# MLP products of a three-layer fp32 kernel by quarters: seven block products instead of eight

## The reference

```python
def squared_relu_mlp(h, w1, w2):
    return jnp.square(jax.nn.relu(h @ w1)) @ w2

mod = (c_act @ ada_w[layer] + ada_b[layer])[:, None, :]
sh_a, sc_a, gt_a, sh_m, sc_m, gt_m = jnp.split(mod, 6, axis=-1)
...
h = modulate(rms_norm(x, mlp_norm[layer]), sh_m, sc_m)
x = x + gt_m * squared_relu_mlp(h, mlp_w1[layer], mlp_w2[layer])
```

## Time and profile before

| what | value |
|---|---|
| three runs | 2585.17, 2585.69, 2588.85 us; median 2585.69 |
| the profiled execution | 2587.35 us, span 2585.6 us |
| mean granted TensorE clock over the span | 0.969 of full |
| TensorE busy | 2444.9 us (95%) |
| VectorE busy | 823.2 us (32%) |
| ScalarE busy | 465.4 us (18%) |
| mlp1 of layer a | first L901 at 381.32, first L959 at 615.50 |
| mlp2 of layer a | first L959 at 615.50, last sum of a chunk followed by the first L393 at 847.34 |

### The profile page before, as it was taken

One profiled execution on the slowest core, in us unless ns is written; L12 is line 12 of the kernel. 1 busy time (PEld: TensorE's weight loads), 2 busy tenths in 40 slices (PEclk: granted clock), 3 DMA queues, 4 the chain that ended last, 5 costly groups with the idle time before them and its releaser, 6 DMA issues. The chain is left out here.

```text
span 2585.6 us, 22377 instructions
## 1 busy us (share of the span) xinstructions
PE 2444.9 (95%) x8264; PEld 1216.3 (47%) x8264; DVE 823.2 (32%) x1835; ACT 465.4 (18%) x995; POOL 42.9 (2%) x50
## 2 busy tenths in 40 slices
PE   6999899999999999989999999999999899998886
PEld 4444544444444645554444444464554643343332
DVE  4444432112122436653211213138642411110104
ACT  2232211110000324441211100021231200000001
POOL 0000000000000000000000000000000000000000
PEclk9999799999999999989999999999999899999998
DMA  8443213333433111112433433341003569999995
GB/s 341 158 168 147 98 65 130 130 130 130 169 157 130 57 65 50 49 74 98 163 130 132 172 151 130 130 163 65 33 1 130 230 266 427 426 426 425 424 422 205
DMA packets 45426, 452.29 MB, mean 175 GB/s; under 512 B 7784, under 2 KB 7784, under 8 KB 20240
## 3 DMA queue, kind: packets, MB, share of 16 engines
q1 hardware_dynamic: 37616, 435.64, 42.0%
q0 software_dynamic: 6528, 12.17, 1.3%
q10 hardware_dynamic: 1184, 3.19, 0.3%
HBM read 444.54 MB, written 18.39 MB: 179 GB/s over the span
## 5 line engine op out<-in xcount | busy, mean ns | idle before, releaser
L959 PE MATMUL ps<-big,ring 128*128 128x512 f32 x1024 | 448.9, 596 | 3.9 <-PEq L871 1.8
L901 PE MATMUL ps<-hT,ring 128*128 128x512 f32 x1024 | 444.3, 594 | 0.0
L959 PEld LDWEIGHTS ps<-big,ring 128*128 128x128 f32 x1024 | 192.6, 191 | 245.9 <-issue 245.9
L901 PEld LDWEIGHTS ps<-hT,ring 128*128 128x128 f32 x1024 | 193.9, 191 | 237.9 <-issue 236.6
L2572 PE MATMUL ps<-ring,big 128*64 128x512 f32 (+1 forms) x768 | 233.3, 614 | 25.2 <-issue 15.3
L512 PE MATMUL ps<-hT,ring 128*128 128x512 f32 x384 | 175.0, 607 | 2.1 <-ACT hT L429 2.1
L2572 PEld LDWEIGHTS ps<-ring,big 128*64 128x64 f32 (+1 forms) x768 | 85.2, 151 | 144.3 <-issue 131.0
L1653 PE MATMUL ps<-hT,ring 128*128 128x512 f32 x320 | 142.4, 600 | 2.7 <-DVE big L2035 1.7
L2572 PE MATMUL ps<-big 128*64 128x512 f32 (+1 forms) x352 | 130.0, 604 | 6.6 <-ACT big L2633 3.3
L207 DVE SCALAR_TENSOR_TENSOR tmp<-ring,cact,tmp 128x512 f32<-128x512 f32 (+1 forms) x192 | 131.6, 685 | 6.8
L856 DVE TENSOR_TENSOR mod<-ps,vec 128x4 f32 (+1 forms) x16 | 2.6, 162 | 367.4 <-PE ps L214 367.4
(11 more groups left out here) (433 smaller groups left out, 2506.6 us busy)
## 6 DMA issues: line engine op xcount, KB each, us to landing
ring<-in_stream SPq DMA_DIRECT2D x99, 2048.0 KB, 8.4
ring<-in_gate SPq DMA_DIRECT2D x17, 2048.0 KB, 29.2
ring<-in_up SPq DMA_DIRECT2D x16, 2048.0 KB, 25.2
ring<-in_down SPq DMA_DIRECT2D x15, 2048.0 KB, 27.4
big<-in_up SPq DMA_DIRECT2D x9, 2048.0 KB, 25.2
big<-in_down SPq DMA_DIRECT2D x8, 2048.0 KB, 27.1
big<-in_gate SPq DMA_DIRECT2D x7, 2048.0 KB, 24.8
hT<-in_down SPq DMA_DIRECT2D x5, 2048.0 KB, 26.5
```

The lines of the kernel that those rows point to most:

```text
L901: last = pe.matmul(m.ps[:, j, :], w[:, k, j * P:(j + 1) * P], m.hT[:, k, :], start=(k == 0), stop=(k == KT - 1))
L959: last = pe.matmul(m.ps[:, bank(half, j), :], w[:, k, j * P:(j + 1) * P], hid[:, 8 * c + k, :], start=(c == 0 and k == 0), stop=(c == 3 an ...
```

## The change

Both products are computed by the Strassen-Winograd scheme on quarters. The two operands are cut in four quarters each; eight products of quarters become seven, and sums of quarters are formed before and after. In the names of the code the quarters of the weights are a11, a12, a21, a22, those of the rows b11, b12, b21, b22; S1, S2, S4 and a changed a21 are sums of weight quarters, T1, T2, T4 and a changed b12 are sums of row quarters; P1 to P7 are the seven products.

In mlp1 the first chunk of w1 is computed as before. Each of the other seven chunks is two pairs; a pair makes two hidden tiles f and g. Each of its seven products is four products of the code with a moving operand of 256 columns (`product`, L937). The sums of rows are formed once, those of weights (S1, S2, a21, S4, 512 elements per partition each) on VectorE for each pair, in place for a21 in the ring. VectorE joins the seven results from PSUM in seven additions of 256 elements. ScalarE copies P1 out of PSUM and does Relu and Square in place on quarters. The eight instructions of a modulation chunk are spread over the two pairs. The loop over four rounds is written out.

In mlp2 a step is one k of a chunk: seven products of two products of the code each, 256 columns, summed in seven banks over the 16 steps of a half. VectorE forms the sums of step s+1 during step s (256 elements each; eight instructions per step in the first half, seven in the second), with two sets of buffers. At the end of a half `outputs` joins the banks in seven additions of 512 elements and applies gate and residual in eight instructions of 256 elements (`joined`). The tiles are then squared in the order 2, 3, 0, 1. Buffers for all this are `oT`, `rs`, and parts of `tmp` and `hT`.

The diff, cut to its core:

```diff
-def square_rows(m, act, sq, scale, j, freed, sqd):
+def square_rows(m, act, sq, scale, j, freed, sqd, tile=None):
+    f = j if tile is None else tile
...
+                def product(name, a, b):
+                    out = m.ps[:, bank[name], 0:H]
+                    for k in range(4):
+                        ins = pe.matmul(out, a[:, k, :], b[:, k, :], start=(k == 0), stop=(k == 3))
+                    ins.then_inc(prod, 1)
...
+                for i, (c, q) in enumerate(pairs):
+                    if i:
+                        pe.wait_ge(p1_ok, i)
+                    product("P1", a11, b11)
+                    pe.wait_ge(s12_ok, i + 1)
+                    if i:
+                        pe.wait_ge(u2_ok, i)
+                    product("P6", s2, t2)
...
+                    product("P5", s1, t1)
+                    if q == 0:
+                        modulation_rows(c - 1)
...
+                    product("P7", a21, b12)
...
+                    product("P2", a12, b21)
...
+                    product("P4", a22, t4)
...
+                    product("P3", s4, b22)
+                    if q == 1:
+                        pe.wait_ge(prod, PRODUCTS * (i + 1))
+                        pe.sem_inc(m.free[chunk1(c)[0]], 1)
+                modulation_rows(7)
...
+                for i, (c, q) in enumerate(pairs):
+                    dve.wait_ge(p1_ok, i + 1)
+                    dve.wait_ge(prod, done + 2)
+                    dve.tensor_tensor(u2, p1, ps("P6"), ALU.add).then_inc(u2_ok, 1)
+                    ada(c, 4 * q, 4 * q + 1)
...
+                    if i + 1 < len(pairs):
+                        sums_a(*pairs[i + 1])
...
+                    dve.tensor_tensor(hid[:, f, H:T], u4, ps("P3"), ALU.add).then_inc(c12, 1)
+                    if i + 1 < len(pairs):
+                        sums_b(*pairs[i + 1], i + 1)
+                    ada(c, 4 * q + 3, 4 * q + 4)
...
+    steps = [(half, c, k) for half in range(2) for c in range(4) for k in range(4)]
+                    def product(name, a, b):
+                        for q in range(2):
+                            ins = pe.matmul(m.ps[:, bank[name], q * H:(q + 1) * H], a[:, q * P:(q + 1) * P], b,
+                                            start=(first and q == 0), stop=(final and q == 1))
+                        ins.then_inc(prod, 1)
...
+                def sums(s):
+                    if s >= 2:
+                        dve.wait_ge(prod, PRODUCTS * (s - 1))
...
+                    if c == 3 and k == 3:
+                        outputs(half)
+                for j in range(4, 7):
+                    squares(j)
```

More of the change, by code:

```diff
@@ L887, in _ @@
             def _(pe):
-                pe.sem_inc(relu, 4)
-                pe.sem_inc(mod_done, 1)
-                keep_busy(m, pe, 5, 7)
[L891 to L908, removed]
@@ new lines, in _ @@
+                keep_busy(m, pe, 5, 7)
+                chunk, full, v = ring_chunk(m, at)
+                pe.wait_ge(full, v)
+                w = chunk.rearrange("p (k n) -> p k n", k=8)
+                for j in range(4):
+                    for k in range(KT):
+                        if j == 0:
+                            pe.wait_ge(h_ok, k + 1)
+                        last = pe.matmul(m.ps[:, j, :], w[:, k, j * P:(j + 1) * P], m.hT[:, k, :],
+                                         start=(k == 0), stop=(k == KT - 1))
+                    last.then_inc(mm, 1)
@@ L910, in _, with squared @@
+                modulation_rows(7)
             @block.scalar
             def _(act):
-                act.sem_inc(sq, 2)
-                shift_rows(act, outs, hs, h_ok)
[L914 to L921, removed]
+                def squared(f, h, n):
+                    part = hid[:, f, h * H:(h + 1) * H]
+                    act.activation(part, part, ACT.Relu).then_inc(flat, 1)
+                    act.wait_ge(flat, n)
+                    act.activation(part, part, ACT.Square)
@@ new lines, in joined @@
+                def joined(f, h):
+                    for q in range(2):
+                        x = m.xT[:, f + q, h * H:(h + 1) * H]
+                        ins = dve.scalar_tensor_tensor(x, cres[:, q * H:(q + 1) * H], gate[:, f + q:f + q + 1], x, ALU.mult, ALU.add)
+                        c1.n += 1
+                        ins.then_inc(chn, 1)
+                        if f % 4 == 2 and h == 0 or f % 4 == 0 and h == 1:
+                            dve.wait_ge(chn, c1.n)
+                            dve.sem_inc(added, 1)
+                    dve.wait_ge(chn, c1.n)
@@ new lines, in squares @@
+                def squares(j):
+                    if 1 <= j <= 6:
+                        add_squares(dve, sq1, j, sqd, freed)
+                        if inner is not None:
+                            add_squares(dve, sq2, j, sqd2, freed2)
+                sums(0)
+                for s, (half, c, k) in enumerate(steps):
+                    if s + 1 < len(steps):
+                        sums(s + 1)
+                    i = 4 * half + c
+                    n2 = at2 + 2 * i + 1
+                    if k == 0:
+                        dve.wait_ge(m.full[n2 % RING], 16 * (n2 // RING + 1))
+                    if k < 3:
+                        ada_steps(dve, c1, n2 % RING, j_par(n2), (0, 3, 6)[k], (3, 6, 8)[k], acc_ready)
+                    if k == 2:
+                        ada_release(dve, n2 % RING, i, acc_ready)
+                    if k == 3:
+                        ada_bias(dve, tiles * (8 + i), i, row_sum, mod_done)
+                    if half and c == 0 and k < 3:
+                        squares(k + 1)
+                    if c == 3 and k == 3:
+                        outputs(half)
```

338 lines of the change are left out of this document (260 added, 78 removed).

## The result

The changed kernel took 2515.68 us, the median of four runs (2514.14 to 2517.10), beside 2585.94 for the kernel before on the same chip. The ratio is 0.9726, with a 95% interval of 0.9714 to 0.9737. The forecast was 2513.5. The profiled execution took 2515.37 us.

The account below looks back on a forecast made before the run. The prediction took TensorE, bound by its columns, as the limit: 2587.35 - 97.7 gained + 25.5 added on the path = 2515.2 us for the profiled execution, 2513.5 on the median, range 2498 to 2544.

Parts of the forecast that it names:

- record of 256 columns: TensorE, both products: 0.217 us each, from a straight line between 0.111 at 128 and 0.4288 at 512 columns.
- gain on 30 chunks: Both products, two layers: 30 x 3.14 = 94.2 us, plus 3.5 from mlp1's modulation rows, sum 97.7 us.
- first pair and first sums: Start of mlp1 and mlp2: TensorE waits about 0.35 and 0.1 us; 0.9 us in two layers.
- end of mlp1: Last join and modulation step precede the last modulation rows: 0.95 us in a, 1.1 in b, 0.85 for b's slow start.
- end of mlp2: VectorE's joins, residuals and squares delay the sums, which run at half clock: 10.0 us in a with next block, 11.7 in b.
- the half's end: Middle of mlp2: joins and residuals delay the next sums on VectorE, hidden by 0.1 us; counted 0, 2 us per layer kept.
- VectorE's load: VectorE about 72% busy in mlp1 and 80% in mlp2, named as a sign that the forecast is right.
- B: Semaphore wait at each product's head, 644 in all, costs 0.05 us; time 2546, chance 0.11.
- C: Each of 644 semaphore waits drains TensorE's queue, 0.50 us each, 322 us; time about 2835, chance 0.04.
- D: VectorE becomes the bound, its two-operand additions taking 1.8 times their rows; time about 2600, chance 0.03.
- F: Better than 2500: 256 columns at 0.2144 us and the idle end at full clock; time 2498, chance 0.03.
- E: Weight loads not hidden on TensorE: 0.11 us more on each of 3360 records, 370 us; time about 2883, chance 0.01.

Follow-up runs that it names:

- E1: Only the second MLP product (mlp2) by quarters, mlp1 as in the kernel before; 2557.21 us, ratio 0.9899 to the kernel before.
- e2: Only the first MLP product (mlp1) by quarters, mlp2 as in the kernel before; 2539.14 us, ratio 0.9826 to the kernel before.
- E3: Changed kernel with the first half's additions of squares one chunk later and mlp1's last modulation steps ahead of the last joins; 2506.40 us.
- e8: Changed kernel with E3's reorderings, e4's fillers, and modulation rows of the second half's first chunk one step later; 2496.32 us.
- e4: Changed kernel with filler products on TensorE during its wait for the squares at the end of mlp2; 2503.83 us.
- e5: Changed kernel with dummy VectorE reductions of 512 elements, four a pair in mlp1, two in nearly every mlp2 step; 2519.16 us.
- e9: e8 with layer a's last four tiles' squares summed by TensorE, not first added on VectorE, and fillers between the runs of sums; 2499.21 us.
- e6: Changed kernel with dummy VectorE reductions of 512 elements, eight a pair in mlp1 and four a step in mlp2; 2642.62 us.

## Why the prediction was right

The time from the start of mlp1 to the block after mlp2 fell by 38.46 us in layer a and by 33.99 in b, 72.45 together. The prediction's sum was 97.7 - 25.5 = 72.2, with 1.0 us of it for the block behind them. Outside them the trace moved by 3 us at most. Term by term:

| term | predicted | measured |
|---|---|---|
| record of 256 columns | 0.217 us | 0.216 |
| a chunk, mlp1 and mlp2 | 25.6 us | 25.61 and 25.45 |
| gain on 30 chunks | 97.7 us | 14 x 3.39 + 16 x 3.30 = 100.3 |
| first pair and first sums, both layers | 0.9 | 0.33 and 0.34 more idle before the first product (0.73 and 0.74, before 0.40) |
| end of mlp1, a and b | 0.95 and 1.1, and 0.85 for the clock | 0.65 and 0.51, no clock lost in b |
| middle of mlp2, a and b | 0, with 2 each kept in the range | 2.20 and 2.39 |
| end of mlp2, a | 9.0, and 1.0 in the next block | 8.8, and nothing in the next block (27.66 us for 64 records, before 27.63) |
| end of mlp2, b | 11.7 | 12.1 |
| first chunk of mlp1, a | no term | 1.07 less: 27.63 us at full clock, before 28.70 |

That the sums agree to 0.3 us is luck. The columns gave 2.6 us more than was counted, the end of mlp1 cost 0.9 less, and two slow starts that were counted, 0.85 and 1.0 us, didn't come; with the faster first chunk these are 6.4 us on one side, against the 4.6 of the middle of mlp2 on the other. The measured rows leave 1.6 us of loss that no row holds. The range, 2498 to 2544, didn't need this luck.

The price of the record was the main term, and the straight line between the 128 and the 512 columns of the earlier trace rows gave it within 0.001 us. E1 and e2, with the same beats, show that this gain is whole in each block.

The step that failed is the half's end, "hidden by 0.1 us". The sums of weights and rows, which the prediction followed, were ready in time: TensorE's wait there is put down to VectorE's modulation step (L872) and not to a sum. It did not follow the other customer of the same queue: the modulation steps of that chunk, with the additions of squares ahead of them, and their row sums that TensorE asks for at k = 2. It cost 4.6 us in two layers. The prediction's range held it, and named a gap at the half's end as a sign against it; the wrong part was its mechanism. E3 shows the mechanism: with the squares one chunk later the gap shrinks in a and goes in b; e8, which asks later, closes it.

At the end of mlp1 the order was right and the size too large, 2.05 us for 1.16: the last modulation step stands behind the last join, but starts 0.34 us after it (585.72 and 586.06), where 0.5 was counted, and the idle time at the start of mlp2 is 0.15 us shorter than before in both layers. The slow start of layer b, given half a chance, didn't come, nor that of the block after mlp2 in a. The prediction read the slow start from an idle time of 1.09 us against 0.74; the runs don't bear that out, since after 0.94 us the changed kernel started slow in layer a and after 0.95 us e4 started at full clock. At the end of mlp2 the sums start 8.06 and 9.73 us after the last product where 7.4 and 9.5 were worked out, and run at 0.213 us each as predicted; in a the last residual ends 5.4 us after the last product (801.05 + 1.12), where 5.3 was worked out, and the three additions of squares and the start of the sums take 2.7 us more, where 2.1 was left for them.

VectorE's load was set too high, at 72 and 80% for 62 and 73%: additions that don't need the one before them start 0.34 us apart (709.37 and 709.71, say), less than the 0.416 that the earlier trace rows show for one. It changed nothing, since it was hidden.

The rivals: that each product's wait costs 0.05 us (B) or a drain (C) falls, since 112 records of 0.216 us and the modulation rows fill a chunk of 25.5 us. VectorE as the bound (D) needed 1.8 times its prices; e5 shows that 83 and 90% are hidden inside a chunk. Faster than 2500 (F) needed 0.2144 us a record and an end of mlp2 at full clock; neither came, and only with e4's fillers did the end run at full clock. Loads that aren't hidden (E): a load is busy 0.190 us and the next product's record starts 0.216 us after the last, so the load lies beside the stream. The rule that the prediction took from the Trainium skill, "TensorE: Matmul & The Clock Gate", section "Part 3: Packing small matmuls — row/col tiling", by which a weight load overlaps a running matmul only when their row groups differ, is not what this trace shows: loads and matmuls, all on all rows, are busy 126.47 and 144.54 of the same 146.10 us. (The section also lets a load go ahead into a background weight buffer; no run here shows whether that is what happens.)

Why the clock stayed up after 2.20 us of idle time in one execution and was at half after the same 2.20 in another of the same code stays open. A seam read from one trace is therefore known to no better than the 1 to 2 us that such a start cost here.

## What to carry to other kernels

Seven products for eight pay in full on an engine that is bound by its columns, if the shorter records are priced from rows of two widths and the adding engine keeps some of its time free in each stretch (10% was enough inside the chunks here, not at the seams). Look then for every customer of the engine that does the joins, not only the new ones: what it owes at each point where TensorE asks, in the order of its queue. Put work that nobody waits for behind what is asked for first, and let TensorE run records of 128 columns through a wait that can't be removed.

## What the runs showed of the hardware

- TensorE's clock can fall while it is busy. During one-column records it fell from 1.00 to 0.53 in e4 (1626 to 1630 us) and to 0.50 in e9; in e8 the same records of layer b ran at full clock for 5.3 us. The fillers of 128 columns ran at 1.00 through 7.8 and 9.6 us.
- The start after a short wait isn't fixed by the program: after 2.20 us of idle time at the same place of the same code, eight records of 256 columns took 1.89 us in one execution (the changed kernel) and 3.38 in another (e4).
- A block of work ahead of the step that another engine waits for can cost more than the queue's length gives: in mlp1 of e6 72 us where 8 were worked out, part of it (3.2 us of records in 6.22) at half clock after each gap.
- Fp32 additions of 256 elements per partition start 0.34 us apart when independent and 0.45 when one needs the other's result (698.27 to 698.61, and 698.61 to 699.06 us).
